# Conditioning and first projection in quarters, V with tokens stationary, and 28 products of a zero row

## The reference, cut to what matters

```python
cond = silu(c)
for i in range(2):
    sh1, sc1, g1, sh2, sc2, g2 = split(cond @ mod_w[i] + mod_b[i], 6)
    h = rms_norm(x, norm_mix_g[i]) * (1 + sc1) + sh1
    y = dsa_attention(h, ...) if i == 0 else s5_layer(h, ...)
    x = x + g1 * y
    h = rms_norm(x, norm_ffn_g[i]) * (1 + sc2) + sh2
    x = x + g2 * conv_ffn(h, ...)
return rms_norm(x, final_g)
```

## Time and profile before

| what | value |
|---|---|
| median of 3 runs | 765.52 us |
| the profiled execution's own time | 767.76 us |
| its span (first to last instruction) | 765.8 us |
| TensorE busy | 727.7 us, 95% |
| DVE busy | 530.4 us, 69% |
| ACT busy | 411.9 us, 54% |
| POOL busy | 127.7 us, 17% |
| mean granted clock of TensorE | 0.984 |
| mean DMA rate | 205 GB/s |

### The profile page before, as it was taken

One profiled execution on the slowest core, in us unless ns is written; L12 is line 12 of the kernel. 1 busy time (PEld: TensorE's weight loads), 2 busy tenths in 40 slices (PEclk: granted clock), 3 DMA queues, 4 the chain that ended last, 5 costly groups with the idle time before them and its releaser, 6 DMA issues.

```text
span 765.8 us, 17216 instructions
## 1 busy us (share of the span) xinstructions
PE 727.7 (95%) x6636; PEld 660.5 (86%) x6636; DVE 530.4 (69%) x897; ACT 411.9 (54%) x682; POOL 127.7 (17%) x120
## 2 busy tenths in 40 slices
PE   4789999999999999999999999989999999999996
PEld 1478999457888999999999799979969999999995
DVE  4756665995488788777867686556567767676665
ACT  4244644565465556675567653325556555555554
POOL 1000000211015343434303254430000000000000
PEclk9799999999999999999999999989999999999998
DMA  8979755696755767667676041008725555555521
GB/s 315 378 272 383 255 190 165 255 406 246 283 215 182 280 187 257 209 238 238 221 260 204 3 138 58 29 29 342 263 73 192 177 183 174 192 191 165 192 83 56
DMA packets 46068, 156.61 MB, mean 205 GB/s; under 512 B 6016, under 2 KB 7312, under 8 KB 46016
## 3 DMA queue, kind: packets, MB, share of 16 engines
q1 hardware_dynamic: 43344, 148.26, 55.2%
q10 hardware_dynamic: 2160, 6.38, 2.2%
q0 software_dynamic: 512, 1.25, 0.4%
HBM read 154.82 MB, written 1.05 MB: 204 GB/s over the span
## 4 chain that ended last, share of the span: by engine, by line
PE 85%; DVE 7%; issue 3%; ACT 3%; POOL 1%; DMA 1%; DVEq 0%; POOLq 0%; ACTq 0%
PE up L368 13%; PE up L370 13%; PE up L369 13%; PE acc L368 9%; PE acc L369 9%; PE acc L370 9%; PE gv L410 5%; DVE wlo L1165 2%; PE misc L469 1%; PE up L752 1%; DVE tmp L1193 1%; PE up L765 1%; PE acc L740 1%; DMA ident<-in_ident 1%; PE acc L498 1%
## 5 line engine op out<-in xcount | busy, mean ns | idle before, releaser
L1165 DVE TENSOR_TENSOR wlo<-raw,whi 128x1024 fp32r<-128x1024 f32 x188 | 252.7, 1358 | 77.2 <-ACT whi L820 70.8
L368 PE MATMUL up<-hh,whi 128*128 128x256 f32 x896 | 255.7, 285 | 1.9 <-DVE hl L1198 1.9
L370 PE MATMUL up<-hh,wlo 128*128 128x256 f32 x896 | 253.5, 283 | 0.0
L369 PE MATMUL up<-hl,whi 128*128 128x256 f32 x896 | 253.5, 283 | 0.0
L820 ACT ACTIVATE whi<-raw 128x1024 fp32r<-128x1024 f32 x185 | 192.5, 1051 | 41.0 <-PE acc L370 26.3
L368 PEld LDWEIGHTS up<-hh,whi 128*128 128x128 f32 x896 | 171.7, 192 | 9.8 <-issue 3.8
L369 PEld LDWEIGHTS up<-hl,whi 128*128 128x128 f32 x896 | 171.8, 192 | 0.0
L370 PEld LDWEIGHTS up<-hh,wlo 128*128 128x128 f32 x896 | 171.8, 192 | 0.0
L1496 DVE SCALAR_TENSOR_TENSOR ffn<-up,conv,ffn 128x254 f32<-128x254 f32 (+1 forms) x176 | 72.7, 475 | 45.6 <-ACT ffn L1015 45.3
L368 PE MATMUL acc<-ah,whi 128*128 128x256 f32 x352 | 99.8, 284 | 0.6 <-DVE wlo L1165 0.6
L369 PE MATMUL acc<-al,whi 128*128 128x256 f32 x352 | 99.6, 283 | 0.0
(11 more groups left out here) (240 smaller groups left out, 920.6 us busy)
## 6 DMA issues: line engine op xcount, KB each, us to landing
raw<-in_w SPq DMA_DIRECT2D x188, 512.0 KB, 3.4
mraw<-in_mw SPq DMA_DIRECT2D x48, 512.0 KB, 6.1
arena<-in_mw SPq DMA_DIRECT2D x24, 512.0 KB, 9.7
raw<-in_w SPq DMA_DIRECT2D x12, 256.0 KB, 13.0
tmp<-in_mw SPq DMA_DIRECT2D x6, 512.0 KB, 7.7
ffn<-in_mw SPq DMA_DIRECT2D x6, 512.0 KB, 8.5
tmp<-in_mw ACTq DMA_DIRECT2D x4, 512.0 KB, 6.0
ffn<-in_mw ACTq DMA_DIRECT2D x4, 512.0 KB, 8.6
```

The lines of the kernel that those rows point to most:

```text
L368: pe.matmul(out, w_h, xh, start=first, stop=False, skip_group_check=skip)
L369: pe.matmul(out, w_h, xl, start=False, stop=False, skip_group_check=skip)
L370: return pe.matmul(out, w_l, xh, start=False, stop=last, skip_group_check=skip)
L1165: dve.tensor_tensor(wlo[:, n % SPL, :], raw[:, n % RAW, :], whi[:, n % SPL, :].bitcast(F32), ALU.subtract).then_inc(lo_ready, 1)
```

## The change

1. **Quarters.** The weights of chunks 0 to 3 are laid out anew: each holds 256 columns of scale and 256 of shift, for two K tiles. Each chunk opens and closes its own accumulation in `gv` and has its own row copy, columns, bias and multiplier (`first_row_out`, `first_columns`, `first_scale`). `quarter(n, c)` multiplies two K tiles of slot n; all six slots are done for c = 0, then 1, 2, 3. SP loads the six first halves ahead of chunk 1. `gemv(C_PROJ)` comes after the last quarter. DVE's table steps and coefficients get other places.
2. **Zero products.** `open_bank(up[:, 1, :])` is issued 14 times ahead of the wait for the constants, 4 times ahead of `gemv(0)`, and 10 times ahead of the first quarters.
3. **V.** The order of the slots is q, v, k. A V slot now holds 128 K rows by all 1024 output channels; the stationary operand is `hh` or `hl` of 128 tokens, the moving one is 512 columns of `whi` or `wlo`, 12 products a slot, accumulating in the four banks of `acc` over eight slots. ACT copies the four banks to `vt` during the first four K slots. The transposes of V, `v_out`, `vsb`, the copies by POOL and `stage` are gone; scores read `qkv` directly, and wait for `sp_ready` of the pair two before instead of `v_ready`. Loops over these slots and over pairs 1 to 4 are unrolled on PE and ACT.

```diff
-S_KI, S_WI, S_QI, S_Q, S_K, S_V = 0, 1, 2, 6, 14, 22
+S_KI, S_WI, S_QI, S_Q, S_V, S_K = 0, 1, 2, 6, 14, 22
...
-            load_early(1)
             for n in range(RAW):
                 load_half(n, 0)
-            load_early(2)
-            load_early(3)
+            for c in range(1, 4):
+                load_early(c)
...
+            def first_columns(c):
+
+                odd = c % 2
+                pe.wait_ge((first_row, gm_ready)[odd], c // 2 + 1)
+                if c:
+                    pe.wait_ge((mod_col, first_col)[odd], (c + 1) // 2)
+                for q in range(4):
+                    mm = pe.matmul(misc[:, q:q + 1], gm[:, q * P:(q + 1) * P], picks[:, 0:1], start=True, stop=True)
+                mm.then_inc((first_cols, cols_done)[odd], 1)
...
-            def half(n, h):
-
-                pe.wait_ge((first_lo, lo_ready)[h], n + 1)
-                for kk in range(4):
-                    k = 4 * h + kk
+            def quarter(n, c):
+
+                pe.wait_ge((first_lo, lo_ready)[c // 2], n + 1)
+                for k in (2 * c, 2 * c + 1):
                     pe.wait_ge(act_lo, k + 1)
+                    kk = k % 4
                     w_h, w_l = whi_half[:, n, kk * P:(kk + 1) * P], wlo_half[:, n, kk * P:(kk + 1) * P]
                     pe.matmul(idx_bank[n], w_h, hh[:, k, :], start=(k == 0), stop=False, skip_group_check=True)
                     pe.matmul(idx_bank[n], w_h, hl[:, k, :], start=False, stop=False, skip_group_check=True)
                     mm = pe.matmul(idx_bank[n], w_l, hh[:, k, :], start=False, stop=(k == KT - 1), skip_group_check=True)
-                mm.then_inc((first_used, slot_used)[h], 1)
+                if c % 2:
+                    mm.then_inc((first_used, slot_used)[c // 2], 1)
 
             pe.wait_ge(set_up, 5)
+            for _ in range(14):
+                open_bank(up[:, 1, :])
             pe.wait_ge(ones_in, 16 * N_ONES)
             norm(0, 0, None)
+            for _ in range(4):
+                open_bank(up[:, 1, :])
             pe.wait_ge(cond_ready, 1)
             gemv(0)
             spread_root(0, misc[:, T:2 * T])
+            first_columns(0)
+            for _ in range(10):
+                open_bank(up[:, 1, :])
+            for n in range(RAW):
+                quarter(n, 0)
             gemv(1)
-            columns(0)
-            half(0, 0)
-            pe.wait_ge(gm_ready, 1)
+            first_columns(1)
             gemv(2)
-            half(1, 0)
-            half(2, 0)
+            for n in range(RAW):
+                quarter(n, 1)
+                if n == 1:
+                    first_columns(2)
             gemv(3)
-            half(3, 0)
-            pe.wait_ge(hp_ready, 4)
-            columns(1)
-            half(4, 0)
-            half(5, 0)
-            for n in range(RAW):
-                half(n, 1)
-                if n == 3:
-                    gemv(C_PROJ)
+            first_columns(3)
+            for c in (2, 3):
+                for n in range(RAW):
+                    quarter(n, c)
+            gemv(C_PROJ)
...
-            with pe.Fori(2, N_IN // RAW) as i:
-                for n in range(RAW):
-                    stream(n, i)
-
+            for n in range(2 * RAW, S_V):
+                stream(n)
 
             pe.wait_ge(idx_relu, 2)
-            pe.wait_ge(qkv_ready, N_IN)
+            for k in range(KT):
+                n = S_V + k
+                pe.wait_ge(lo_ready, n + 1)
+                for b in range(2):
+                    x_h, x_l = hh[:, k, b * P:(b + 1) * P], hl[:, k, b * P:(b + 1) * P]
+                    for tokens, w in ((x_h, whi), (x_h, wlo), (x_l, whi)):
+                        for f in range(2):
+                            mm = pe.matmul(acc[:, 2 * b + f, :], tokens, w[:, n % SPL, f * 512:f * 512 + 512],
+                                           start=(k == 0 and tokens is x_h and w is whi),
+                                           stop=(k == KT - 1 and tokens is x_l))
+                mm.then_inc(slot_used, 1)
+            for n in range(S_K, N_IN):
+                pe.wait_ge(qkv_ready, n - KT - 1)
+                project(up[:, n % 2, 0:T], n)
+            pe.wait_ge(vt_ready, 4)
+            pe.wait_ge(qkv_ready, N_IN - KT)
 
             def scores(p, a):
-                pe.wait_ge(stage_ready, 6 if isinstance(p, int) and p < 2 else 3 * (p + 1))
-                if not (isinstance(p, int) and p < 2):
-                    pe.wait_ge(v_ready, p - 1)
+                if p >= 2:
+                    pe.wait_ge(sp_ready, 2 * p - 2)
                 for e in range(2):
-                    r = HD * e
-                    pe.matmul(acc[:, 2 * a + e, 0:T], stage[r:r + HD, a, 0, P:T], stage[r:r + HD, a, 1, :],
-                              start=True, stop=True)
-                    pe.matmul(acc[:, 2 * a + e, T:T + P], stage[r:r + HD, a, 0, 0:P], stage[r:r + HD, a, 1, 0:P],
-                              start=True, stop=True)
-                for kt in range(2):
-                    mm = pe.transpose(acc[:, 2 * a + kt, 384:512], stage[:, a, 2, kt * P:(kt + 1) * P], ident[:])
+                    q, k = (qkv[HD * e:HD * e + HD, s + p, :] for s in (S_Q, S_K))
+                    pe.matmul(acc[:, 2 * a + e, 0:T], q[:, P:T], k, start=True, stop=True)
+                    mm = pe.matmul(acc[:, 2 * a + e, T:T + P], q[:, 0:P], k[:, 0:P], start=True, stop=True)
                 mm.then_inc(s_done, 1)
...
+            def first_row_out(c):
+
+                odd = c % 2
+                act.wait_ge(mod_used, MS * (c + 1))
+                if c:
+                    act.wait_ge((cols_done, first_cols)[odd], (c + 1) // 2)
+                act.activation(gm[:], gv[:], ACT.Copy).then_inc((first_row, gm_ready)[odd], 1)
+
             act.wait_ge(csum, 1)
-            row_out(0)
+            first_row_out(0)
             first_half(0, 0)
             first_half(1, 0)
-            act.wait_ge(mod_col, 1)
-            for k in range(4):
-                first_in(k)
+            first_in(0)
+            first_in(1)
             for n in range(2, RAW):
                 first_half(n, 0)
-            row_out(1)
-            first_half(0, 1)
-            first_half(1, 1)
-            act.wait_ge(mod_col, 2)
-            for k in range(4, KT):
-                first_in(k)
-            for n in range(2, RAW):
+            for c in (1, 2):
+                first_row_out(c)
+                first_in(2 * c)
+                first_in(2 * c + 1)
+            first_row_out(3)
+            for n in range(RAW - 1):
                 first_half(n, 1)
+            first_in(6)
+            first_in(7)
+            first_half(RAW - 1, 1)
...
-            with act.Fori(2, N_IN // RAW) as i:
-                for n in range(RAW):
-                    tile_out(n, i)
+            for n in range(2 * RAW, S_V):
+                tile_out(n)
+            for n in range(S_V, S_K):
+                split_hi(n + SPL)
+            for n in range(S_K, N_IN):
+                tile_out(n)
+                if n < S_K + 4:
+                    act.activation(vt[:, (n - S_K) // 2, (n % 2) * 512:(n % 2) * 512 + 512], acc[:, n - S_K, :],
+                                   ACT.Copy).then_inc(vt_ready, 1)
...
+            def first_scale(c):
+
+                odd = c % 2
+                dve.wait_ge((first_cols, cols_done)[odd], c // 2 + 1)
+                dve.tensor_tensor(modc[:, 4 * c:4 * c + 4], misc[:, 0:4], modb[:, 4 * c:4 * c + 4],
+                                  ALU.add).then_inc((first_col, mod_col)[odd], 1)
+                dve.wait_ge((first_col, mod_col)[odd], c // 2 + 1)
+                dve.scalar_tensor_tensor(amul[:, 0, 2 * c:2 * c + 2], modc[:, 4 * c:4 * c + 2], 1.0,
+                                         gains[:, 0, 2 * c:2 * c + 2], ALU.add,
+                                         ALU.mult).then_inc((first_amul, amul_ready)[odd], 1)
+                dve.wait_ge((first_amul, amul_ready)[odd], c // 2 + 1)
...
-            for h in range(2):
-                if h:
-                    coefficients()
-                    assert np_[0] == PRM_STEPS
-                    tab_step(dve.tensor_scalar(turns, turns, 0.25, None, ALU.add))
-                    tab_step(dve.tensor_scalar(tcos, turns, ROUND, -ROUND, ALU.add, ALU.add))
-                col_out(h)
-                first_scale(h)
-                first_scaled(4 * h)
-                first_half(0, h)
-                first_low(4 * h)
-                for k in range(4 * h + 1, 4 * h + 4):
-                    first_scaled(k)
-                    first_low(k)
-                for n in range(1, RAW):
-                    first_half(n, h)
+            first_scale(0)
+            scaled(0, 0)
+            first_half(0, 0)
+            scaled(0, 1)
+            first_low(0)
+            first_half(1, 0)
+            first_low(1)
+            for n in range(2, RAW):
+                first_half(n, 0)
+            coefficients()
+            assert np_[0] == PRM_STEPS
```

(43 more changed lines are left out.)

100 lines of the change are left out of this document (38 added, 62 removed).

## The result

The changed kernel takes 769.25 us (median of 6 runs, 768.13 to 770.67) where the kernel before takes 765.88 (6 runs, 765.27 to 766.80): a ratio of 1.004, interval 1.0024 to 1.0055. It is 3.4 us slower, where 9.9 us of gain were forecast. Its profiled execution took 769.56, near its median; that of the kernel before was 1.9 above its own, so the two traces differ by only 1.8, and 1.6 of the 3.4 us lie between executions. A slower kernel had been given a chance of 0.05.

The account below looks back on a forecast made before the run. TensorE, busy 95% of the span, was taken as the bound, with waits and half clock in the front. Gains of 6.0 (front), 1.9 (V) and 2.0 (attention) sum to 9.9 us, off the 765.52 median: 755.6, range 753.0 to 761.0.

Parts of the forecast that it names:

- The step that failed: Front's start: 14 zero products, six dense microseconds at half clock, raise TensorE's clock, mostly held; gemv(0) takes 1.8 us.
- Rival 2: Front: one-row zero products don't raise the clock at all; front gain 0, kernel at 761.6 us; chance 0.15.
- The four products ahead of `gemv(0)`: Front's start: four zero products cost 0.9 us before gemv(0), which ends at about 16.3 us.
- first quarter: Front, start of the first pass: first quarter's product at 20.0 us, after columns of 0.5 us.
- The first pass: Front, six slots times the first two K tiles: from 20.0 us to 24.6 us.
- Third pass: Front, after gemv(3): starts at 39.5 us, paced by DVE to 44.6 us.
- The wait behind the loads: Before the seventh slot: four ACT load issues (2.03 us) and a 0.38 us copy leave TensorE idle 2.5 us, to 53.3.
- forecast gain of 6.0: Front: seventh slot moves from 59.28 to 53.3 us, a gain of 6.0 us.
- V: Eight V slots: 12 products of 512 columns at 0.22 us replace 24 at 0.12; gain 1.9 us, range 0 to 2.4.
- Attention: Attention stage: dropped transposes and copies of V gain 2.0 us, bounds 0.65 to 3.3; turns 5.4 us apart.
- three signs of being wrong: Clock row falls inside the passes, seventh slot starts after 57 us, or wide products stand 0.24 us or more apart.

Follow-up runs that it names:

- v_only: The kernel before with only the new slot order, tokens-stationary V and attention stage, old front in halves: 763.01 us, ratio 0.9955 to the kernel before.
- warm_zero_128rows: The changed kernel with its 28 extra products on 128 rows of zeros instead of one row: 763.73 us, ratio 0.9959 to the kernel before.
- front_only: The kernel before with only the quarters and the 28 zero-row products, V as before: 772.89 us, ratio 1.0087 to the kernel before.
- one_row_of_ones: The changed kernel with its 28 extra products on one row of ones instead of zeros: 769.56 us, ratio 1.0052 to the kernel before.
- no_zero_products: The changed kernel without its 28 zero-row products: 765.80 us, ratio 0.9992 to the kernel before.
- warm_ones_128rows: The changed kernel with its 28 extra products on 128 rows of ones instead of one zero row: 762.80 us, ratio 0.9951 to the kernel before.
- ones_and_act_order: warm_ones_128rows with ACT's copies of the fifth and sixth tiles ahead of the loads waiting for gemv(4): 759.39 us, ratio 0.9913 to the kernel before.
- third_pass_early: ones_and_act_order with six second halves split earlier and the third pass freed from first_columns(3): 755.57 us, ratio 0.9883 to the kernel before.

## Why the prediction was wrong

**The step that failed** is in the front's start: "I forecast that six dense microseconds raise the clock in the same way and that it is mostly held." They were dense (6.15 us without a gap), and did not raise it: each took 0.44 us to the last. The ground was `gemv(0)`, which raises the clock with 2 of 128 columns in use; but it has all 128 rows. The 14 products raise the clock with zeros or ones in 128 rows, and don't with zeros or ones in one row. Nor was it "mostly held": it fell behind the ten, behind 1.64 us and behind 2.91 us of waiting. Rival 2 named this mechanism and its doubt (no row of the trace shows one) and had a chance of 0.15; its replay has the end of `gemv(0)` at 19.2 and the third pass at 45.6, and the trace shows 19.0 and 46.18. The 28 products with 128 rows give 6 to 7 of the 13.65 us back; the rest is in the sizes below.

**The sizes behind it.** Even rival 2's 761.6 was 7.7 too low, and the seventh slot at 59.4 came at 61.58.
- The four products ahead of `gemv(0)` cost 1.9 instead of 0.9, `gemv(0)` 3.6 instead of 1.8. `columns` with one moving column takes 1.0 us, not 0.5: 3.5 us at the first quarter (23.49 against 20.0).
- The first pass ran from 23.5 to 26.8 at half clock: 1.5 us, 5.0 at its end (29.6 against 24.6).
- Third pass: forecast at 39.5, came at 46.18, 6.7 late. `gemv(3)` already started 6.0 late, at 40.85 instead of 34.9: 5.0 from the first pass, and 1.0 added by the second, with its waits of 0.74 and 0.36. Between `gemv(3)` and the pass lies a chain of copy, columns (1.05), scaling and a weight half that TensorE waits for in two places (0.74 and 1.64); its links were taken too short, by 0.7 in all. Behind the second wait the clock is at 0.50 to 50.8; passes three and four take 10.6 us (46.18 to 56.77) instead of 9.4.
- The wait behind the loads was forecast at 2.5 (ending at 53.3) and measured at 2.91, with 2.4 in the kernel with ones. Its mechanism held, and the loads' new place took some 3 us off. What I left out is its possible sequel: in this trace the whole seventh slot ran at 0.50, which costs it 2.65 us more; with 128 rows in the extra products it did not follow. At its end the front stands 4.95 later than before, 10.95 from the forecast gain of 6.0.

**V.** Forecast 1.9 with 0.22 per product; measured 0.227 and 1.2. The same 0.013 us stand over the columns' time at 256 columns (0.120 - 0.107) and at 512 (0.227 - 0.213). The Trainium skill (TensorE: Matmul & The Clock Gate, Back-to-back issue gap) gives an isolated product of 512 columns 216 ns. The fp32r products here, each with its own load of the stationary operand (PE and PEld both have x6568), stand 11 ns further apart, so for them the trace decides against that figure.

**Attention.** Forecast 2.0, measured 2.5 in the changed kernel (139.05 to 206.76 is 67.7 us against 70.2) and 1.55 in `v_only`. Turns 5.4 apart were forecast; they are 5.2 to 5.8. V and attention together, forecast at 3.9, gave 3.5 by the ratio of `v_only` and 4.2 by its medians; the traces have 2.9 there and 3.6 in the changed kernel. V's part was 0.7 too high and attention's 0.5 too low in the changed kernel, so that the sum comes out is in part luck.

**The sum.** 10.95 in the front, 0.7 in V, -0.5 in attention, 0.6 behind the norm and 1.9 between the profiled executions and the medians (767.76 stands 2.2 above the 765.52 on which the forecast was built, 769.56 stands 0.3 above 769.25) add up to the 13.65 us between 755.6 and 769.25, to within 0.1.

**The signs.** Two of the prediction's three signs of being wrong came: the clock row falls inside the passes, and the seventh slot starts after 57. The third, wide products 0.24 apart, did not.

**What the change was good for** also came out: with 128 rows in the extra products, the loads' and the third pass's places mended, the kernel runs at 755.57. That this equals the forecast number is chance in part: its seventh slot starts at 49.94, 3.4 us ahead of the forecast 53.3, and V gives less than forecast.

## What to carry to other kernels

A product meant to raise TensorE's clock should use all 128 rows, as those that did here; check it by the duration of the next dense work, and don't trust that a busy engine is a fast one. When a wait of one to three microseconds opens on TensorE, count its length and then the half-clock stretch that may follow: 2.65 us behind a wait of 2.91 in the changed kernel, nothing behind 2.94 in `warm_zero_128rows`. One trace doesn't tell whether the next execution pays it. Before a step is moved, look at what stands behind it in the issuing engine's order: here the copy behind four load issues was worth some 3 us and the unneeded wait for the fourth chunk's columns 2 to 4.

## What the runs showed of the hardware

- 14 back-to-back bf16 products of 512 columns with one row in use ran at 0.44 us each for 6.15 us and left the clock where it was, in all five kernels that have them; with 128 rows, zeros or ones, they took 4.74 to 5.83 us in all in the five kernels that have those, because the clock rose within them. The Trainium skill (TensorE: Matmul & The Clock Gate, Part 1: The HAM clock gate) tells the clock by how busy the engine has been; by the profile it was fully busy in both forms, so busy time alone doesn't tell it here.
- The granted clock of the windows and the pace can disagree: 16 to 18 us reads 1.00 while `gemv(0)` runs at 3.60 us, nearly twice its 1.90. Every window of that trace before 22 us reads 1.00, also the first, in which TensorE has not begun. In the first 20 us the duration of a known product is the better witness.
- Ten one-row products don't hold a clock that is up: at full pace (2.33 us) they were followed by 0.50 in the changed kernel, and in `front_only` they slowed down themselves (3.34 us). Ten with 128 rows (2.32 us) were followed by full pace.
- The length of a wait alone doesn't tell whether the clock falls. Behind the 1.64 us ahead of the third pass it fell in each kernel that has that wait. Ahead of the seventh slot it fell behind waits of 2.57 us (`one_row_of_ones`) to 3.89 (`no_zero_products`) in six kernels, and not behind 2.38 (`warm_ones_128rows`) and 2.94 (`warm_zero_128rows`). Behind waits of 0.30 or 0.29 and twice 0.83 us it fell in the kernel before and not in `v_only`. Ahead of the norm TensorE waited 1.99 us in `ones_and_act_order` and 1.98 in `third_pass_early`; the four products behind the norm then took 1.87 us at half clock in the first and 1.02 at full in the second.
- The clock also moves far from the change. Every trace has a stretch at 0.50 near 500 us, at places of the work that differ; between 501.0 and 502.5 `v_only` gains 1.0 us on the kernel before by it. So a difference of about 1 us between two of these kernels need not come from where their code differs.
